# Splitting the row-norm sums and reordering the opening of the feed-forward network in a PE-bound decoder step

## The chip, the cores and the metric

The kernel runs on one core of one Trainium2 chip. The metric is the device time of one execution in microseconds (us). Engines are named as in the profile: PE (TensorE matmul), PEld (its weight loads), DVE (VectorE), ACT (ScalarE), POOL (GpSimd) and SP (the engine that issues most of the DMAs).

## The reference: what is computed

One inference step for 1024 prompt tokens and 32 new tokens (8 sequences of 4), so R = 1056 rows of width D = 1024, float32. Layer 0 is a spatial-gating layer, layer 1 a stick-breaking attention layer; each is followed by a SwiGLU network with 2816 hidden columns. Every sub-layer is preceded by an RMSNorm.

```python
def rmsnorm(x, g):
    r = lax.rsqrt(jnp.mean(xf * xf, axis=-1, keepdims=True) + NORM_EPS)
    return (xf * r).astype(x.dtype) * g

def swiglu(x, wg, wu, wd):
    return (jax.nn.silu(x @ wg) * (x @ wu)) @ wd

def sgu_mixer(xn, w_in, v_g, ws, bs, w_out, chunk_len):
    z = jax.nn.gelu(xn @ w_in, approximate=False)
    u, v = jnp.split(z, 2, axis=-1)
    v = rmsnorm(v, v_g)
    ...
    s = jnp.einsum('gts,bnsgd->bntgd', w, vc) + bs[:, :chunk_len].T[None, None, :, :, None]
    y = (u * s.reshape(B, T, D_MODEL)) @ w_out
```

## The kernel before

**Layout.** Activations lie transposed: 128 features on the partitions, the 1056 rows along the free dimension, eight such tiles for D. Each product is done in three matmuls with split operands (high times high, high times low, low times high), so a tile of 128 output features over 1056 rows is 8 x 3 x 3 = 72 matmuls of 352 columns in `project_from` (L1146). The five engines run five hand-written instruction lists, each strictly in order, tied by counting semaphores (`wait_ge`). PSUM has six banks `ps` (two sets of three) and two banks `aux`.

**Row norms.** The squares of a row lie over 8 x 128 features. ACT squares the tiles, DVE adds the eight squared tiles up in `scratch`, PE sums over the partitions by a matmul with `neg_ones`, 352 columns each, three of them (`row_sums`, the matmul is L1160), alternating between the two `aux` banks. ACT takes the square root of each back into `scratch` (`rms`, L1823, which gives `aux_out`), and DVE takes the reciprocal. As there are two `aux` banks, `aux_free` makes the third sum wait for ACT's first square root. Each of these sums is float32 and shows in the trace as two matmul records.

**The spatial-gating layer.** PE makes tiles 0 to 7 (the v half), then tile 8 (u of group 0), then `row_sums(1)`, tile 9 (u of group 1, bank set 1), tile 10 (u of group 2, bank set 0), then `v_to_rows(0)` and `v_to_rows(1)`: transposes of the normalised v of a group into `aux` in three rounds (L1171 eight transposes in two rounds, L1173 the last), which ACT copies away (`rows_out`, L1832 and L1835); then `spatial` of group 0, which writes bank set 1. DVE's list here is: `scaled_out(8)` (L2446), the reciprocal `r_v` (L2440), eight instructions L2480 that scale the eight v tiles (two big inputs, `v_all` and `r_v`, both in SBUF), then `scaled_out(9)`, `scaled_out(10)`. ACT's list: `gelu_u(0)`, `rms(1)`, `gelu_u(1)`, which waits for `scaled_out(9)`, and only then the copies of `v_to_rows(0)`. The third round of `v_to_rows(0)` needs the copy of its first.

**POOL's weight slabs.** POOL splits each weight slab in three instructions (L1018, L1019, L1022, inputs in SBUF). There are two slots: the slab for tile 11 + x overwrites the slot of a tile that is done, so the split of the next u slab begins as soon as PE ends tile 9, and the one after it as soon as PE ends tile 10.

**The feed-forward network.** It is done in units u = 0, 1, 2, ... (gate and up alternate), each as seven half-size products m = 1 to 7 (a Strassen-like scheme). `product(u, m, bank, fresh)` is 4 x 2 x 3 = 24 matmuls of 264 columns (L1318) into one of four bank pairs; weights come from a ring of seven slots, whose sums DVE makes (`turn_1` to `turn_4`, L2599 to L2619; for the first units `turn_2_alone`, L2635 and L2636), ACT rounds (`part_high`, L1969) and POOL subtracts (`part_low`, L1065). The right-hand sides of m = 5, 6, 7, 3 are sums S1 to S4 of activations that DVE makes in the opening (`q11_made`, `s2_made` L2812, `s3_made` L2819, `s4_made` L2825), ACT rounds (`s_high`, L1989) and DVE subtracts (`s_low`, L2833). DVE also evacuates the banks: `c11_scaled` (L2770), `t6_added` (L2742), `t3_added` (L2747), `c22_added` (L2755), `c12_added` (L2775). In the opening, `product(0, 6)` waits for `c11_scaled(0)`, `product(1, 6)` for `c11_scaled(1)`, `product(0, 7)` for `t6_added(0)`, and `product(2, 6)` for the weight sum that ACT rounds behind `s_high` of S4, tile 2. The opening runs twice, once per layer, with row sums 2 and 4.

Of the kernel before, what the change touches and what calls it, by code (L numbers as in the profile page):

```python
# [33 lines left out]
NC = 3  # L34
CH = R // NC
# [13 lines left out]
Q_SGU, Q_WOUT = 0, 16  # L49
# [27 lines left out]
X_NORM = [3 + 2 * RT + 1]  # L77
# [117 lines left out]
def parted_at(layer, u, m):  # L195

    return NPR * layer + PARTS.index((u, m)) + 1
# [53 lines left out]
def s_low_at(layer, x, j):  # L251

    return 4 * HK * layer + S_LOWS.index((x, j)) + 1
# [21 lines left out]
def a_ready(layer, n):  # L275

    return (2 + 3 * layer) * KT + max(h_order(layer).index(x) for x in range(n + 1)) + 1
# [17 lines left out]
def yoco_step(nc, x_prompt, x_sample, cache_k, cache_v, page_table, norm_mix_g, a_w_in, a_v_g, a_ws, a_bs, a_w_out,  # L295
# [4 lines left out]
    with ExitStack() as ctx:  # L300
        def sb(name, shape, dt=F32, where=ctx):
            return where.enter_context(nc.sbuf_tensor(name, shape, dt))

        def sem(name):
            return ctx.enter_context(nc.semaphore(name))
# [20 lines left out]
        scratch = sb("scratch", [P, R])  # L326
# [13 lines left out]
        neg_ones = sb("neg_ones", [P, P])  # L340
# [36 lines left out]
        in_hi = sb("in_hi", [P, KT, R], F32R, far)  # L377
        in_lo = sb("in_lo", [P, KT, R], F32R, far)
# [87 lines left out]
        aux = ctx.enter_context(nc.psum_tensor("aux", [P, 2, TB], F32))  # L466
# [18 lines left out]
        aux_done = sem("aux_done")  # L485
# [107 lines left out]
        def slot(q):  # L593

            return w_hi[:, q % 2], w_lo[:, q % 2]
# [15 lines left out]
        def ring_slot(layer, u, m):  # L611

            n = PARTS.index((u, m)) % RING
            if n < 4:
                return ring_own[layer][:, n, 0], ring_own[layer][:, n, 1]
            if n < 6:
                x = (w_hi, w_lo)[n - 4][:, last_slot(layer)]
                return x[:, 0:HW], x[:, HW:2 * HW]
            return ring_last[layer][:, 0], ring_last[layer][:, 1]
# [17 lines left out]
        def moving_of(layer, m):  # L637

            if m in (1, 2, 4):
                x = (1, 2, 4).index(m)  # L640
                return A_HI[layer][:, x], A_LO[layer][:, x]
            return s_parts(layer, {5: 1, 6: 2, 7: 3, 3: 4}[m])
# [477 lines left out]
        def _(pe):  # L1120
            mm = nc.tensor.matmul

            def bank_free(t):

                if not isinstance(t, int) or t >= 2:
                    pe.wait_ge(tile_out, t - 1)

            def project(t, par, q, slab, first_input=None, source=(in_hi, in_lo)):

                pe.wait_ge(w_ready, q + 1)  # L1130
                project_from(slot(slab), t, par, first_input, source)

            def project_from(parts, t, par, first_input=None, source=(in_hi, in_lo)):

                bank_free(t)
                hi, lo = parts
                out = ps[:, 3 * par:3 * par + 3, :]
                for k in range(KT):
                    if first_input == 40:
                        pe.wait_ge(in_ready, 40 + max(O_ORDER.index(n) for n in range(k + 1)) + 1)  # L1140
                    elif first_input is not None:
                        pe.wait_ge(in_ready, first_input + k + 1)
                    ks = slice(k * P, k * P + P)
                    for c in range(NC):
                        for n, (w, x) in enumerate(((hi, source[0]), (hi, source[1]), (lo, source[0]))):
                            last = mm(out[:, c, 0:CH], w[:, ks], x[:, k, c * CH:c * CH + CH],  # L1146
                                      start=(k == 0 and n == 0), stop=(k == KT - 1 and n == 2))
                last.then_inc(tile_done, 1)

            def aux_free(x):  # L1150
                if not isinstance(x, int) or x >= 2:
                    pe.wait_ge(aux_out, x - 1)

            def row_sums(event):

                pe.wait_ge(sq_added, KT * event)
                for c in range(NC):
                    x = X_NORM[event] + c
                    aux_free(x)
                    mm(aux[:, x % 2, 0:CH], neg_ones[:], scratch[:, c * CH:c * CH + CH],  # L1160
                       start=True, stop=True).then_inc(aux_done, 1)

            def to_rows(src, x, par):

# [15 lines left out]
            for r in range(RT):  # L1180
                pe.wait_ge(x_in_s[r], 16)
                for n in range(2):
                    x = X_ROWS + 2 * r + n
# [6 lines left out]
            x = X_ROWS + 2 * RT  # L1190
# [8 lines left out]
            for n in range(2):  # L1199
                x = X_WS + n  # L1200
# [5 lines left out]
            near_in = (near_hi, near_lo)  # L1206
# [3 lines left out]
            for rnd in range(NC):  # L1210
                x = X_NORM[0] + rnd
# [8 lines left out]
                for c in range(2):  # L1220
                    project(2 * i + c, c, Q_SGU + 2 * i + c, Q_SGU + c, source=near_in)
            project(8, 0, Q_SGU + 8, Q_SGU + 8, source=near_in)
            row_sums(1)
            project(9, 1, Q_SGU + 9, Q_SGU + 9, source=near_in)

            def v_to_rows(g, par):
                pe.wait_ge(v_normed, g + 1)
# [71 lines left out]
            def ffn(layer, event, t_before):  # L1299
                t0 = T_FFN[layer]  # L1300
                pairs = (ps[:, 0:2], ps[:, 2:4], ps[:, 4:6], aux[:, 0:2])

                def product(u, m, bank, fresh):

                    pe.wait_ge(part_ready, parted_at(layer, u, m))
                    hi, lo = ring_slot(layer, u, m)
                    x_hi, x_lo = moving_of(layer, m)
                    for k in range(HK):
                        if u < 2 and m == 1:
                            pe.wait_ge(in_ready, a_ready(layer, k))  # L1310
                        elif u < 2 and m in (2, 4):
                            pe.wait_ge(in_ready, a_ready(layer, HK + k))
                        elif u < 2:
                            pe.wait_ge(s_ready, s_low_at(layer, {5: 1, 6: 2, 7: 3, 3: 4}[m], k))
                        ks = slice(k * P, k * P + P)
                        for c in range(2):
                            for n, (w, x) in enumerate(((hi, x_hi), (hi, x_lo), (lo, x_hi))):
                                last = mm(pairs[bank][:, c, 0:QC], w[:, ks], x[:, k, c * QC:c * QC + QC],  # L1318
                                          start=(fresh and k == 0 and n == 0), stop=(k == HK - 1 and n == 2),
                                          skip_group_check=True)  # L1320
                    last.then_inc(mult_done, 1)
# [11 lines left out]
                product(0, 1, 0, True)  # L1333
                pe.wait_ge(tile_out, t_before + KT)
                product(1, 1, 1, True)
                row_sums(event)
                product(0, 4, 2, True)
                pe.wait_ge(aux_out, X_NORM[event] + NC)
                product(1, 4, 3, True)
                copied(0)  # L1340
# [441 lines left out]
            for i, n in enumerate(O_ORDER):  # L1782
# [11 lines left out]
                for k in range(first_k, KT):  # L1794
# [4 lines left out]
                    for m, (w, x) in enumerate(((hi, in_hi), (hi, in_lo), (lo, in_hi))):  # L1799
                        for c in range(NC):  # L1800
                            last = mm(out[:, c, 0:CH], w[:, ks], x[:, k, c * CH:c * CH + CH],  # L1801
                                      start=(k == first_k and m == 0), stop=(k == KT - 1 and m == 2))
# [613 lines left out]
        def _(dve):  # L2416
# [34 lines left out]
            for r in range(RT):  # L2451
                for n in range(2):
                    x = X_ROWS + 2 * r + n
# [3 lines left out]
            x = X_ROWS + 2 * RT  # L2457
# [157 lines left out]
            def turn_3(layer, u):  # L2615

                b11, b21, b12, b22 = sources(layer, u)
                dve.wait_ge(turned_done, turned_sum(layer, u, 6 if u < 2 else 5))
                vec.tensor_tensor(b12, b22, b12, ALU.subtract).then_inc(turned_done, 1)  # L2619
# [10 lines left out]
            def turn_2_alone(layer, u):  # L2630

                b11, b21, b12, b22 = sources(layer, u)
                x = ring_sum(layer, u, 6)
                ring_wait(layer, u, 6)
                step_done(vec.tensor_tensor(x, b12, b11, ALU.subtract))  # L2635
                vec.tensor_tensor(x, b22, x, ALU.subtract).then_inc(turned_done, 1)  # L2636
# [48 lines left out]
            def ffn(layer, event, first_in):  # L2685
                t0 = T_FFN[layer]
                r1, ratio, r2 = r_row[:, 0:H2], r_row[:, H2:R], scratch[:, H2:R]
                a, b, c, d = (ps[:, 0:2, 0:QC], ps[:, 2:4, 0:QC], ps[:, 4:6, 0:QC], aux[:, 0:2, 0:QC])
# [78 lines left out]
                def c11_scaled(u, p12):  # L2767
                    a21_read(u, 0)
                    done(u, 2)
                    vec.tensor_tensor(c_of(u, 0), p12, halved(r1), ALU.mult).then_inc(evac, 1)  # L2770
# [56 lines left out]
                def s_low(x, j):  # L2827
                    dve.wait_ge(s_hi_done, s_part_at(layer, x, j))
                    if x == 2:
                        dve.wait_ge(s_ready, s_low_at(layer, 1, j))  # L2830
                    hi, lo = s_parts(layer, x)
                    src = s_sum(layer, 4 if x == 2 else x, j)
                    vec.tensor_tensor(lo[:, j, :], src, as32(hi[:, j, :]), ALU.subtract).then_inc(s_ready, 1)  # L2833
# [4 lines left out]

                for j in range(HK):
                    s_low(1, j)  # L2840
                for j in range(HK):
                    q11_made(j)
                    s2_made(j)
                    if j > 0:
                        s_low(2, j - 1)
                turn_2_alone(layer, 1)
                s_low(2, HK - 1)
                c11_scaled(0, a)
                turn_3(layer, 0)
                s3_made(0)  # L2850
                c11_scaled(1, b)
                turn_3(layer, 1)
                t1_scaled(0)
                t1_scaled(1)
# [63 lines left out]
                for i in range(FP - 1):  # L2918
                    for n in range(KT):
                        t = t0 + KT * i + n  # L2920
# [427 lines left out]
```

## Time and profile before

| | us |
|---|---|
| median of 3 runs | 2614.57 (2613.02 to 2615.01) |
| the profiled execution, its time | 2614.33 |
| its span, first to last instruction | 2612.5 |
| PE busy | 2525.5 (97%) |
| DVE, ACT, POOL busy | 1698.9, 1000.5, 978.7 |
| mean granted TensorE clock | 0.992 |

The span is 1.8 us shorter than the execution's own time. PE is busy nearly all the time, so only a stretch in which PE stands or runs at the lower clock can be won back, and any new one is paid in full.

### The profile page before, as it was taken

Reading aid. Unit: us, or ns where it says so; the run is one execution under the profiler, and the core shown is the slowest. Engines: PE = TensorE matmul, PEld = TensorE weight load, DVE = VectorE, ACT = ScalarE, POOL = GpSimd, SP = SyncE. Lnnn points to the kernel's source line nnn. Section 1 sums busy time; section 2 is a strip of 40 time slices with the busy share of each in tenths; the row PEclk is TensorE's granted clock in tenths of the full one; section 3 lists DMA queues with packets and bytes.
Section 4 is the critical chain, followed back from the end, with each engine's and each line's share of the span. In section 5 each row is a group of like instructions: output and inputs, shape, how many; then the busy total and the mean of one; then the engine's idle time right before and its main releaser. Section 6 shows DMA issues by size and latency. Waiting matters only on the chain.

```text
span 2612.5 us, 44346 instructions
## 1 busy us (share of the span) xinstructions
PE 2525.5 (97%) x17835; PEld 2411.5 (92%) x17835; DVE 1698.9 (65%) x1937; ACT 1000.5 (38%) x1480; POOL 978.7 (37%) x616
## 2 busy tenths in 40 slices
PE   8999989999999999999999999999989999999997
PEld 7989988999999999988888888879889999999997
DVE  4244497556666766778788878885785545567565
ACT  4222153222221111377777777774432222221113
POOL 4643435878985876000000000000245555552110
PEclk9999999999999999999999999999999999999999
DMA  4111223544445664422222231244222222234211
GB/s 132 42 42 34 74 76 96 174 151 158 152 146 216 221 219 152 152 86 84 82 74 80 89 99 61 88 129 160 82 82 82 66 88 77 82 139 162 94 66 75
DMA packets 271134, 284.93 MB, mean 109 GB/s; under 512 B 14810, under 2 KB 213778, under 8 KB 270930
## 3 DMA queue, kind: packets, MB, share of 16 engines
q1 hardware_dynamic: 252770, 272.79, 31.8%
q10 hardware_dynamic: 18160, 9.31, 1.2%
q8 instruction: 141, 2.31, 0.4%
q14 instruction: 63, 0.52, 0.1%
HBM read 195.37 MB, written 86.67 MB: 108 GB/s over the span
## 4 chain that ended last, share of the span: by engine, by line
PE 73%; DVE 10%; issue 3%; ACT 2%; POOL 1%; DMA 1%; ACTq 0%; SPq 0%; DVEq 0%; POOLq 0%
PE ps L1318 24%; PE ps L1407 16%; PE aux L1536 8%; PE aux L1318 4%; PE ps L1146 4%; PE ps L1453 3%; PE ps L1481 3%; PE ps L1435 2%; PE ps L1801 2%; PE ps L1465 2%; DVE s_lo L2833 1%; PE aux L1500 1%; PE aux L1547 1%; DVE h L2924 1%; DVE sp_part_odd L2984 1%
## 5 line engine op out<-in xcount | busy, mean ns | idle before, releaser
L1318 PE MATMUL ps<-s_hi,ring 128*128 128x264 f32 x2016 | 382.0, 287 | 19.1 <-DVE h L2770 8.0
L1065 POOL TENSOR_TENSOR ring<-w_raw,ring 128x512 fp32r<-128x512 f32 x44 | 79.2, 1799 | 844.4 <-ACT ring L1969 844.4
L1318 PEld LDWEIGHTS ps<-s_hi,ring 128*128 128x128 f32 x2016 | 320.4, 191 | 21.7 <-DVE h L2770 8.4
L1407 PE MATMUL ps<-s_hi 128*128 128x352 f32 x1008 | 326.8, 324 | 11.2 <-DVE h L2932 4.5
L1407 PE MATMUL ps<-s_hi,s_lo 128*128 128x352 f32 x1008 | 325.1, 323 | 0.0
L1407 PE MATMUL ps<-s_lo,s_hi 128*128 128x352 f32 x1008 | 323.7, 321 | 0.0
L1318 PE MATMUL ps<-s_lo,ring 128*128 128x264 f32 x1008 | 288.9, 287 | 0.0
L2932 DVE TENSOR_TENSOR h<-h,ps 128x1056 f32<-128x1056 f32 x144 | 180.3, 1253 | 144.2 <-PE ps L1407 142.9
L1065 POOL TENSOR_TENSOR ring<-ring_plain,ring 128x512 fp32r<-128x512 f32 x90 | 132.6, 1491 | 270.4 <-DVE w_hi_plain L2613 228.4
L1969 ACT CAST ring<-ring_plain 128x512 fp32r<-128x512 f32 x90 | 52.0, 621 | 435.4 <-DVE ring_plain L2606 432.7
L1407 PEld LDWEIGHTS ps<-s_hi 128*128 128x128 f32 x1008 | 189.0, 187 | 16.0 <-DVE h L2932 7.9
L1318 PEld LDWEIGHTS ps<-s_lo,ring 128*128 128x128 f32 x1008 | 193.4, 192 | 0.0
L1146 PE MATMUL ps<-near_hi,w_hi 128*128 128x352 f32 x576 | 187.3, 325 | 4.7 <-DVE near_lo L2423 4.7
L1407 PEld LDWEIGHTS ps<-s_hi,s_lo 128*128 128x128 f32 x1008 | 190.4, 189 | 0.0
L1407 PEld LDWEIGHTS ps<-s_lo,s_hi 128*128 128x128 f32 x1008 | 189.6, 188 | 0.0
L2003 ACT CAST s_hi<-a_plain 128x2112 fp32r<-128x2112 f32 x22 | 43.3, 1967 | 381.0 <-PE ps L1407 335.2
L1146 PE MATMUL ps<-near_hi,w_lo 128*128 128x352 f32 x576 | 187.3, 325 | 0.0
L1146 PE MATMUL ps<-near_lo,w_hi 128*128 128x352 f32 x576 | 187.2, 325 | 0.0
L1536 PE MATMUL aux<-in_hi,w_hi 128*128 128x384 f32 (+1 forms) x528 | 172.7, 327 | 1.5 <-issue 0.7
L1536 PE MATMUL aux<-in_lo,w_hi 128*128 128x384 f32 (+1 forms) x528 | 170.3, 322 | 0.0
L1536 PE MATMUL aux<-in_hi,w_lo 128*128 128x384 f32 (+1 forms) x528 | 169.8, 322 | 0.0
L1318 PE MATMUL ps<-a_hi,ring 128*128 128x264 f32 x736 | 142.4, 286 | 4.0 <-DVE h L2770 3.5
(386 smaller groups left out, 6843.9 us busy)
## 6 DMA issues: line engine op xcount, KB each, us to landing
hid_kept<-h SPq DMA_DIRECT2D x44, 528.0 KB, 6.1
a_plain<-hid_kept SPq DMA_DIRECT2D x44, 528.0 KB, 5.5
w_raw<-in_w_gate_dram SPq DMA_DIRECT2D x44, 512.0 KB, 4.9
w_hi<-kept_hi SPq DMA_DIRECT2D x30, 512.0 KB, 4.0
w_lo<-kept_lo SPq DMA_DIRECT2D x30, 512.0 KB, 5.3
h_kept<-h SPq DMA_DIRECT2D x24, 528.0 KB, 3.4
h<-h_kept SPq DMA_DIRECT2D x24, 528.0 KB, 6.4
w_raw<-in_w_down_dram SPq DMA_DIRECT2D x24, 512.0 KB, 4.4
```

The source lines that it names most:

```text
L1065: gp.tensor_tensor(lo, src, as32(hi), ALU.subtract).then_inc(part_ready, 1)
L1146: last = mm(out[:, c, 0:CH], w[:, ks], x[:, k, c * CH:c * CH + CH], start=(k == 0 and n == 0), stop=(k == KT - 1 and n == 2))
L1318: last = mm(pairs[bank][:, c, 0:QC], w[:, ks], x[:, k, c * QC:c * QC + QC], start=(fresh and k == 0 and n == 0), stop=(k == HK - 1 and n = ...
L1407: last = mm(out[:, c, 0:CH], w[:, ns], x[:, c * CH:c * CH + CH], start=(f == 0 and m == 0), stop=(f == 1 and m == 2))
L1435: last = mm(ps[:, e, c0:TB], kq[rows, c, kn, P * j:P * j + P], kq[rows, c, qn, TB * b + c0:TB * b + TB], start=(m == 0), stop=(m == 2 and ...
L1453: last = mm(ps[:, 2 + e, c0:TB], neg_tri_r[:], sp_parts[s % 2][:, x, e, c0:TB], start=(first and x == 0), stop=(x == 1), skip_group_check= ...
L1465: last = mm(ps[:, 2 + e, c0:TB], neg_rest_r[:], sp_parts[s % 2][:, x, e, c0:TB], start=False, stop=(x == 1), skip_group_check=True)
L1481: last = mm(ps[:, 4 + e, c0:TB], v_part[:, j, 2 * e:2 * e + 2, :].rearrange("p n d -> p (n d)"), a_part[:, x, e, c0:TB], start=(first and ...
L1536: last = mm(xb[:, 0:CW[chunk]], w[:, ks], x[:, k, cols], start=(k == 0 and m == 0), stop=(k == KT - 1 and m == 2), skip_group_check=True)
L1801: last = mm(out[:, c, 0:CH], w[:, ks], x[:, k, c * CH:c * CH + CH], start=(k == first_k and m == 0), stop=(k == KT - 1 and m == 2))
L1969: nc.scalar.copy(hi, src).then_inc(part_hi, 1)
L2932: vec.tensor_tensor(chunks(h[:, n, :]), chunks(h[:, n, :]), out, ALU.add).then_inc(tile_out, 1)
```

## The change

Two edits. First, `row_sums` can now issue two of its three sums, and the third is issued from inside the product that follows: in tile 9 of the spatial-gating layer before k = 3 (after 27 of its 72 matmuls), and in `product(0, 4)` of both feed-forward openings before k = 2 (after 12 of its 24). Row sums 3 stay as they are. Second, in DVE's list of the feed-forward opening `c11_scaled(0)` and `turn_2_alone(1)` go from behind the S2 rounds to ahead of them, and `turn_3(0)` goes behind `c11_scaled(1)`.

```diff
-            def project_from(parts, t, par, first_input=None, source=(in_hi, in_lo)):
+            def project_from(parts, t, par, first_input=None, source=(in_hi, in_lo), sum_within=None):
...
                 for k in range(KT):
+                    if sum_within is not None and k == 3:
+                        row_sum(sum_within, 2)
...
-            def row_sums(event):
+            def row_sum(event, c):
+
+                x = X_NORM[event] + c
+                aux_free(x)
+                mm(aux[:, x % 2, 0:CH], neg_ones[:], scratch[:, c * CH:c * CH + CH],
+                   start=True, stop=True).then_inc(aux_done, 1)
+
+            def row_sums(event, count=NC):
 
                 pe.wait_ge(sq_added, KT * event)
-                for c in range(NC):
-                    x = X_NORM[event] + c
-                    aux_free(x)
-                    mm(aux[:, x % 2, 0:CH], neg_ones[:], scratch[:, c * CH:c * CH + CH],
-                       start=True, stop=True).then_inc(aux_done, 1)
+                for c in range(count):
+                    row_sum(event, c)
...
-            row_sums(1)
-            project(9, 1, Q_SGU + 9, Q_SGU + 9, source=near_in)
+            row_sums(1, 2)
+            project(9, 1, Q_SGU + 9, Q_SGU + 9, source=near_in, sum_within=1)
...
-                def product(u, m, bank, fresh):
+                def product(u, m, bank, fresh, sum_within=None):
...
                     for k in range(HK):
+                        if sum_within is not None and k == 2:
+                            row_sum(sum_within, 2)
...
-                row_sums(event)
-                product(0, 4, 2, True)
+                row_sums(event, 2)
+                product(0, 4, 2, True, sum_within=event)
...
                 for j in range(HK):
                     s_low(1, j)
+                c11_scaled(0, a)
+                turn_2_alone(layer, 1)
                 for j in range(HK):
                     q11_made(j)
                     s2_made(j)
                     if j > 0:
                         s_low(2, j - 1)
-                turn_2_alone(layer, 1)
                 s_low(2, HK - 1)
-                c11_scaled(0, a)
-                turn_3(layer, 0)
                 s3_made(0)
                 c11_scaled(1, b)
+                turn_3(layer, 0)
                 turn_3(layer, 1)
```

## Rows read from the trace of the kernel before

**Rows 1.** The page, busy time of each engine

```profile
PE 2525.5 (97%) x17835; PEld 2411.5 (92%) x17835; DVE 1698.9 (65%) x1937; ACT 1000.5 (38%) x1480; POOL 978.7 (37%) x616
```

**Rows 2.** PE's waits, whole span: total us, times, longest

```profile
PE ps L1318 <- DVE h L2770: 11.5, 8, 4.0
...
PE aux L1160 <- ACT scratch L1823: 5.6, 3, 3.1
...
PE aux L1173 <- ACT sgu_row L1832: 2.4, 8, 0.3
```

**Rows 3.** PE's timeline between tiles 8 and 9: start, us, engine, line

```profile
134.11 1.35 PE L1160 MATMUL aux<-scratch,neg_ones 128*128 128x352 f32 x4
138.61 0.88 PE L1160 MATMUL aux<-scratch,neg_ones 128*128 128x352 f32 x2 [3.15 <-ACT scratch L1823]
```

**Rows 4.** Windows after it: PE, PEld, DVE, ACT, POOL busy, clock, DMA

```profile
138.60:139.60 1.00, 0.99 (x4) 0.78 (x5) 0.00 (x0) 0.48 (x2) 1.00 (x1) 0.86 0.00 0
139.60:140.60 1.00, 1.00 (x5) 1.00 (x5) 0.49 (x1) 0.98 (x2) 1.00 (x1) 0.50 0.00 0
...
142.60:143.60 1.00, 1.00 (x8) 1.00 (x7) 1.00 (x1) 0.00 (x0) 0.00 (x0) 0.94 1.10 331
```

**Rows 5.** DVE's timeline over tiles 9 and 10

```profile
140.10 6.75 DVE L2440 RECIPROCAL r_v<-scratch 128x1056 f32<-128x1056 f32 x1 [4.54 <-ACT scratch L1823]
146.89 15.34 DVE L2480 SCALAR_TENSOR_TENSOR v_all<-v_all,gains,r_v 128x1056 f32<-128x1056 f32 x8
162.16 1.25 DVE L2446 TENSOR_TENSOR ev<-ps,r_row 128x1056 f32<-128x1056 f32 x1
164.19 1.26 DVE L2446 TENSOR_TENSOR ev<-ps,r_row 128x1056 f32<-128x1056 f32 x1 [0.78 <-PE ps L1146]
```

**Rows 6.** ACT's timeline over the same stretch

```profile
139.52 0.55 ACT L1823 ACTIVATE scratch<-aux,eps 128x352 f32<-128x352 f32 x1 [0.52 <-PE aux L1160]
...
163.44 1.10 ACT L1878 ACTIVATE u_t<-ev 128x1056 f32<-128x1056 f32 x1 [22.07 <-DVE ev L2446]
164.53 1.07 ACT L1832 COPY sgu_row<-aux 128x512 f32<-128x512 f32 x2
```

**Rows 7.** PE's timeline behind tile 10

```profile
163.89 1.03 PE L1171 MATMUL aux<-ident,v_all 128*128 128x128 f32 x8
165.16 0.28 PE L1173 MATMUL aux<-ident,v_all 128*32 128x128 f32 x1 [0.24 <-ACT sgu_row L1832]
```

**Rows 8.** POOL's timeline over tiles 9 to 11

```profile
152.68 2.21 POOL L1018 TENSOR_TENSOR w_hi<-w_raw,gains 128x1024 fp32r<-128x1024 f32 x1 [12.06 <-PE ps L1146]
154.85 2.91 POOL L1019 TENSOR_TENSOR w_raw<-w_raw,gains 128x1024 f32<-128x1024 f32 x1
157.84 3.28 POOL L1022 TENSOR_TENSOR w_lo<-w_raw,w_hi 128x1024 fp32r<-128x1024 f32 x1
164.20 1.90 POOL L1018 TENSOR_TENSOR w_hi<-w_raw,gains 128x1024 fp32r<-128x1024 f32 x1 [3.08 <-PE ps L1146]
```

**Rows 9.** Line L2480 in two narrow windows: ns min/median/max, start

```profile
L2480 DVE SCALAR_TENSOR_TENSOR v_all<-v_all,gains,r_v x1: 1314/1314/1314, 149.4 to 149.4; 128x1056 f32<-128x1056 f32 x1
...
L2480 DVE SCALAR_TENSOR_TENSOR v_all<-v_all,gains,r_v x1: 2947/2947/2947, 155.9 to 155.9; 128x1056 f32<-128x1056 f32 x1
```

**Rows 10.** Windows: the layer-0 opening in two parts, and behind tile 10

```profile
336.00:385.30 49.30, 44.05 (x315) 42.59 (x314) 48.34 (x50) 30.78 (x47) 18.27 (x13) 0.97 0.15 44
385.90:402.30 16.40, 10.15 (x73) 9.00 (x72) 16.12 (x23) 4.69 (x8) 5.38 (x4) 1.00 0.50 128
...
165.10:171.00 5.90, 4.98 (x38) 4.19 (x38) 1.77 (x4) 2.65 (x8) 5.21 (x3) 1.00 0.02 6
```

**Rows 11.** PE's timeline in the layer-0 opening, two of its waits

```profile
378.52 0.59 PE L1318 MATMUL ps<-s_hi,ring 128*128 128x264 f32 x1 [4.04 <-DVE h L2770]
...
402.35 0.56 PE L1318 MATMUL ps<-s_hi,ring 128*128 128x264 f32 x1 [2.88 <-POOL ring L1065]
```

**Rows 12.** DVE's timeline in the layer-0 opening

```profile
377.77 0.70 DVE L2770 TENSOR_TENSOR h<-ps,r_row 128x528 f32<-128x528 f32 x1
```

More of the change, by code:

```diff
@@ L1126, in bank_free, with project @@
                     pe.wait_ge(tile_out, t - 1)
-            def project(t, par, q, slab, first_input=None, source=(in_hi, in_lo)):
+            def project(t, par, q, slab, first_input=None, source=(in_hi, in_lo), sum_within=None):
                 pe.wait_ge(w_ready, q + 1)
-                project_from(slot(slab), t, par, first_input, source)
-            def project_from(parts, t, par, first_input=None, source=(in_hi, in_lo)):
+                project_from(slot(slab), t, par, first_input, source, sum_within)
+            def project_from(parts, t, par, first_input=None, source=(in_hi, in_lo), sum_within=None):
                 bank_free(t)
```

## The prediction

> **What bounds the kernel now.** I read four views in this order. The page first: PE is busy for 97% of the span [rows 1], so the question is only which of its few stops the change touches, and what ends each. The list of waits names them [rows 2]: three stops of together 5.6 us at the third row sum (L1160, behind ACT's first square root), 11.5 us behind `c11_scaled`, the longest 4.0 us, which is the opening of layer 0, and eight small ones at L1173. Then the timelines of all engines around each stop, because what counts is not who ends the stop but who would end the next one. Last the windows, for the clock.
>
> At the spatial-gating site PE stands for 3.15 us before the third sum [rows 3]. Right after it the granted clock falls to 0.50 (1.2 GHz) [rows 4]: the slice from 138.6 shows 0.86, so the fall lies (1 - 0.86)/0.5 = 0.28 us ahead of its end, at 139.3; the slice from 142.6 shows 0.94, so the rise lies 0.12 us behind its start, at 142.7; the three between show 0.50 (one stands in the group). PE loses half of these 3.4 us, 1.7 us. Taken alone, the edit gives back 3.15 + 1.7 = 4.85 us here and 5.6 - 3.15 = 2.45 us in the two openings.
>
> But see what runs beside it. DVE works without a pause from 140.10 to 163.41 [rows 5]: reciprocal, eight scalings, `scaled_out(9)`. ACT's gelu waits 22.07 us for that last one [rows 6], the copies stand behind the gelu in ACT's list, and PE's third round of transposes waits for the first copy, 0.24 us, at 165.16 [rows 7]. So PE reaches this point already 0.24 us before DVE and ACT let it on. The DVE chain bounds this stretch together with PE; an earlier PE gains nothing here.
>
> **The change part by part: spatial-gating site.** (a) PE's gain up to the end of tile 10: tile 9 is done when POOL starts, at 152.68; tile 10 took 164.20 - 152.68 = 11.52 us [rows 8], that is 0.16 us for each of its 72 matmuls. After the change tile 9 ends at 152.68 - 4.85 = 147.8, tile 10 at 159.35.
>
> (b) The third sum is late. It stood at 138.61. Tile 9 now starts where the first two sums end, about 135.3 (134.11 and four passes, the 1.35 us of the row less the overlap), and the sum comes after 27 x 0.16 = 4.3 us, at 139.6. ACT starts its root 139.52 - 138.61 = 0.91 us behind [rows 3, 6], at 140.5. The reciprocal and all behind it start 1.0 us later. Bounds: 0.7 and 1.4 us, for the end of the sums and the passes in a full pipe.
>
> (c) The collision. An L2480 takes 1.31 us alone and 2.95 us while POOL splits a slab [rows 9]; POOL's L1018 takes 1.90 us when DVE does L2446 and 2.21 us beside L2480 [rows 8]. Neighbours overlap by 0.07 us (146.89 + 15.34 = 162.23, and the next starts at 162.16 [rows 5]), so the free pitch is 1.31 - 0.07 = 1.24 us and eight would take 9.9; they take 15.3. One slab split costs the chain the difference, 5.4 us. Before, exactly one of the two splits fell inside the chain: the first, 152.68 to 161.1. The second started at 164.20, behind the last L2480. After the change the first starts at 147.8, still inside (scalings from 140.10 + 1.0 + 6.79 = 147.9, so again 5.4 us). The chain would then end at 163.2; but the second split now starts at 159.35, with (163.2 - 159.35)/1.24 = 3.1 scalings to go. These three meet its three instructions: another 5.4 us. If the arrival is slightly later in the chain, only two are hit: 2/3 of it, 3.6 us. No hit at all: 0. I take 5.4, as three still fit and in the first split the waiting POOL instruction went ahead of the next scaling.
>
> The Trainium skill, page "SBUF — State Buffer", section "Who interferes with whom", says that a DVE instruction with two SBUF inputs and a GpSimd instruction that reads SBUF exclude one another for a whole instruction, and that one with a single SBUF input does not take part. The trace agrees, with 2.95 against 1.31 us in [rows 9] and an L2446 of 1.26 us (one input in PSUM) beside the split at 164.20. By that rule too, the edit worsens this stretch.
>
> (d) So `scaled_out(9)` ends at 163.41 + 1.0 + 5.4 = 169.8, and gelu, copy and PE's third round move with it: PE resumes 6.4 us later than before, at 171.6 instead of 165.16. Its first eight transposes end at 159.35 + 1.0 = 160.4, so it stands for about 11 us.
>
> (e) The clock. A stop of 3.15 us was followed by 3.4 us at 1.2 GHz [rows 3, 4]; an 11 us stop should be followed by at least as much. The next 5.9 us hold 4.98 us of PE work [rows 10], so half speed is nearly all felt: 1.7 us. Bounds: 0.5 (ACT's copies set the pace) and 3.4 (twice as long).
>
> Sum for this site: 1.0 + 5.4 + 1.7 = 8.1 us slower. Behind it PE is the bound until the opening, so it stays.
>
> **Openings.** (f) The third sum inside `product(0, 4)`: PE gains 1.2 us each. (g) `c11_scaled(0)` used to start at 377.77 and PE's stop ended at 378.52 [rows 11, 12]; it now starts some 9 us earlier. But from 336.0 to 385.3 DVE is busy 48.3 of 49.3 us, and from 385.9 to 402.3 16.1 of 16.4 [rows 10]: a closed queue, with the short dip at 385.6 where it waits for ACT behind `turn_3(1)`. The edit changes the order in that queue, not its sum. `turn_3(1)` ends where it did, so do `t6_added(0)`, which frees `product(0, 7)`, and `s4_made(2)`, behind which ACT and POOL make the weight part that ends PE's stop of 2.88 us at 402.35 [rows 11]. PE's 4.04 us before `product(0, 6)` and the 1.2 us come back as a longer stop before `product(0, 7)`. `product(0, 6)` now also meets the low parts of S2 as they come. Worth: 0. What hides it is DVE's queue; without it the gain would be the rivals' 1.2 + 4.0 us an opening.
>
> (h) Small costs in the queue: `c11_scaled(0)` and `(1)` (one input in PSUM) used to run under POOL's `part_low`; now `s3_made(0)` or the `t1_scaled` meet it, up to 0.6 us an opening, and `s_low(2, 3)` waits some 0.2 us for ACT, as nothing stands between it and `s2_made(3)` any more. I take 0.3 us an opening, 0.6 for the two; bounds -0.5 and +1.5 each, for the clock phase behind 402.35 as well. The second opening shows the same pattern (one of two rows shown).
>
> No DMA is moved and SP's list is unchanged; POOL's is unchanged in order, only its start times move.
>
> **Sum.** 8.1 + 0.6 = 8.7 us. The profiled execution took 2614.33 us, span 2612.5; that makes 2623.0. The median is 0.24 us above it: 2623.3.
>
> **Rivals.** (A) The naive one: PE is the only bound, and its stops vanish. 4.85 + 2.45 = 7.3 us, with `c11_scaled` 8.0 more: 2607.3 down to 2599. For it: PE's 97%. Against it: ACT's 22.07 us wait for DVE and the 0.24 us at L1173. It decides if the copies can come over 1.4 us before 165.16, which ACT's order forbids. It is the case of the other sign. 4%.
> (B) The late sum alone: the second split doesn't meet the scalings (it is late, or the exclusion is looser). 1.0 + 1.7 + 0.6 = 3.3 us: 2617.9. It decides if tile 10 ends behind 162. 14%.
> (C) Two of three scalings are hit: 1.0 + 3.6 + 1.7 + 0.6 = 6.9: 2621.5. 22%.
> (D) The openings do gain, some 1.2 us each, as DVE's queue is not quite closed, on top of my loss: 8.1 - 2.4 = 5.7: 2620.3. 10%.
> (E) The edit does nothing at all that counts: the stops are refilled and the second split harms nothing: 2614.6 to 2616. 5%.
> My own case, 2623.3: 45%.
>
> **Chances and range.** The measurement can tell some 0.2%, 5.2 us, from no change; that threshold is 2619.8. Slower: my case, C and most of D, 0.74. Same: B, E and the rest, 0.22. Faster: A, 0.04. The range takes in C and D, most of B, and above my case the 1.7 us more for the clock and about 1.5 us in the openings: 2617.5 to 2626.5.
>
> **What would show it.** PE has no stop between the L1160 at 134.11 and tile 9; the L1160 inside tile 9 at about 139.6; the last root at 140.5; DVE's eight L2480 take about 20.7 us instead of 15.34, six of them near 2.95 us; POOL's second L1018 starts at about 159.4 and is stretched; PE's stop at L1173 is about 11 us, followed by a clock of 0.50. In the openings the stop before `product(0, 6)` shrinks to under 1 us, the one before `product(0, 7)` grows to some 5 us, and the stretch from tile 7 of the projection to the stop at `product(2, 6)` keeps its length within 1 us. I am wrong if eight L2480 take under 18 us, if PE passes L1173 before 167, or if the openings get shorter.

## The result and the profile after

The changed kernel takes 2625.36 us (median of 6 runs, 2621.45 to 2628.5) against 2614.3 us (6 runs) before; the ratio is 1.0041 with a 95% interval of 1.003 to 1.0052. It is slower by 11.1 us by the medians and by 10.7 us by the ratio; forecast were 8.7 us, 2623.3 us, with a range of 2617.5 to 2626.5. The profiled execution of the changed kernel took 2627.2 us, so its trace has some 2 us that the median has not.

In the new file the lines are shifted: `project_from` is L1148, the transposes are L1177 and L1179, ACT's copies of them L1840, the eight scalings L2488, the evacuations L2454, the products L1326, `c11_scaled` L2778, `t6_added` L2750, the roots L1831. In the experiments the numbers are those of the old or of the new file, or one more.

**The spatial-gating site.** PE's timeline in the changed kernel answers to [rows 3, 7]:

```profile
134.40 1.35 PE L1160 MATMUL aux<-scratch,neg_ones 128*128 128x352 f32 x4
135.32 0.59 PE L1148 MATMUL ps<-near_hi,w_hi 128*128 128x352 f32 x1
...
139.91 0.75 PE L1160 MATMUL aux<-scratch,neg_ones 128*128 128x352 f32 x2
...
159.22 1.03 PE L1177 MATMUL aux<-ident,v_all 128*128 128x128 f32 x8
...
171.59 0.39 PE L1179 MATMUL aux<-ident,v_all 128*32 128x128 f32 x1 [11.34 <-ACT sgu_row L1840]
```

The stop of 3.15 us is gone, tile 9 follows the two sums at once, and the third sum sits inside it. PE is through with tile 10 at 159.2 instead of 163.9. And then it stands for 11.34 us. What it waits for is read from ACT, DVE and POOL in turn; ACT's timeline, answering to [rows 6]:

```profile
140.70 0.56 ACT L1831 ACTIVATE scratch<-aux,eps 128x352 f32<-128x352 f32 x1 [1.40 <-PE aux L1160]
...
169.97 1.08 ACT L1886 ACTIVATE u_t<-ev 128x1056 f32<-128x1056 f32 x1 [27.42 <-DVE ev L2454]
170.97 1.05 ACT L1840 COPY sgu_row<-aux 128x512 f32<-128x512 f32 x2
```

DVE's, answering to [rows 5]:

```profile
141.29 6.75 DVE L2448 RECIPROCAL r_v<-scratch 128x1056 f32<-128x1056 f32 x1 [5.43 <-ACT scratch L1831]
148.08 20.70 DVE L2488 SCALAR_TENSOR_TENSOR v_all<-v_all,gains,r_v 128x1056 f32<-128x1056 f32 x8
168.70 2.41 DVE L2454 TENSOR_TENSOR ev<-ps,r_row 128x1056 f32<-128x1056 f32 x2
```

And POOL's, answering to [rows 8]:

```profile
148.01 1.90 POOL L1018 TENSOR_TENSOR w_hi<-w_raw,gains 128x1024 fp32r<-128x1024 f32 x1 [7.08 <-PE ps L1148]
149.86 2.91 POOL L1019 TENSOR_TENSOR w_raw<-w_raw,gains 128x1024 f32<-128x1024 f32 x1
152.85 3.29 POOL L1022 TENSOR_TENSOR w_lo<-w_raw,w_hi 128x1024 fp32r<-128x1024 f32 x1
159.53 1.95 POOL L1018 TENSOR_TENSOR w_hi<-w_raw,gains 128x1024 fp32r<-128x1024 f32 x1 [3.38 <-PE ps L1148]
161.44 2.90 POOL L1019 TENSOR_TENSOR w_raw<-w_raw,gains 128x1024 f32<-128x1024 f32 x1
164.42 3.23 POOL L1022 TENSOR_TENSOR w_lo<-w_raw,w_hi 128x1024 fp32r<-128x1024 f32 x1
```

Both slab splits now lie beside the scalings (148.08 to 168.78), and the second and third instruction of each are stretched alike; before, the second split began at 164.20 with DVE's scalings done. The scalings take 20.70 us, not 15.34. The windows behind the stop show the clock, answering to [rows 4] (PE, PEld, DVE, ACT and POOL busy, clock, DMA share, GB/s):

```profile
160.30:166.00 5.70, 0.00 (x0) 0.00 (x0) 5.70 (x3) 0.00 (x0) 5.62 (x3) 0.76 0.00 0
166.00:171.50 5.50, 0.00 (x0) 0.00 (x0) 5.11 (x3) 1.52 (x3) 1.66 (x1) 0.50 0.33 95
171.50:173.40 1.90, 1.63 (x7) 1.36 (x8) 0.00 (x0) 0.88 (x4) 0.00 (x0) 0.50 0.03 9
173.40:177.00 3.60, 3.60 (x19) 3.37 (x18) 0.00 (x0) 1.21 (x3) 0.00 (x0) 0.51 0.02 5
177.00:179.00 2.00, 1.80 (x14) 1.40 (x13) 1.19 (x2) 0.52 (x2) 0.00 (x0) 1.00 0.00 0
```

The first window, at 0.76, holds the fall, some 3 us into the stop. The clock stays at 0.50 (1.2 GHz) for the rest of the stop and for the first 5.5 us behind it, to 177.

**The opening of layer 0.** PE's stops there, answering to [rows 11]:

```profile
382.30 0.36 PE L1326 MATMUL ps<-s_hi,ring 128*128 128x264 f32 x1 [0.78 <-DVE s_lo L2841]
384.25 0.39 PE L1326 MATMUL ps<-s_hi,ring 128*128 128x264 f32 x1 [1.00 <-DVE s_lo L2841]
386.30 0.39 PE L1326 MATMUL ps<-s_hi,ring 128*128 128x264 f32 x1 [1.06 <-DVE s_lo L2841]
389.55 0.39 PE L1326 MATMUL ps<-s_hi,ring 128*128 128x264 f32 x1 [1.45 <-DVE h L2778]
...
397.10 0.59 PE L1326 MATMUL ps<-s_hi,ring 128*128 128x264 f32 x1 [4.37 <-DVE h L2750]
...
411.79 0.36 PE L1326 MATMUL ps<-s_hi,ring 128*128 128x264 f32 x1 [2.89 <-POOL ring L1065]
```

Before, the stop in front of `product(0, 7)` was a short one:

```profile
387.69 0.39 PE L1318 MATMUL ps<-s_hi,ring 128*128 128x264 f32 x1 [1.68 <-DVE h L2742]
```

The one stop of 4.04 us before `product(0, 6)` is cut up: three short ones at its start and inside it, together 2.84 us, each on the next tile of S2's low part, then one of 1.45 us on `c11_scaled(1)`; and the stop before `product(0, 7)` grows from 1.68 to 4.37 us. The last one, at `product(2, 6)`, is as long as before (2.88). Measured from DVE's addition of tile 6 (336.14 before, 344.64 after, L2680 in the new file) it comes after 67.15 us instead of 66.21; in the second opening, after 67.13 instead of 66.14.

**Where the time went**, each stretch between the same two instructions of both traces: from the evacuation of tile 8 (134.31, now 134.60) to the addition of tile 6 before the first opening 8.2 us more; the first opening 0.9 us, the second 1.0 us. That is 10.1 of the 12.0 us between the spans; 0.3 lies ahead of tile 8. The remaining 1.6 us lie where the two programs are the same: 0.5 between the openings (from the stop at `product(2, 6)` to the addition of tile 6 in layer 1: 1447.9 before, 1448.4 after) and 1.1 behind the second (696.1 and 697.2). Over all nine traces of this document these two stretches take 1445.6 to 1450.8 and 695.5 to 697.9 us, and the program is the same there in all of them. So nothing shows that the 1.6 us belong to the change, and sums over the edited stretches are a firmer measure than the spans.

### The profile page after: what moved, and what is told of

Its sections match the earlier page's. It is cut to its first block, busy times and chain, and to the rows that moved or that the text cites. A ratio compares the mean times of both kernels' runs of the same rounds, so it can differ in the third digit from the quotient of the medians.

```text
span 2624.5 us, 44346 instructions
## 1 busy us (share of the span) xinstructions
PE 2530.0 (96%) x17835; PEld 2417.4 (92%) x17835; DVE 1705.8 (65%) x1937; ACT 1001.1 (38%) x1480; POOL 983.2 (37%) x616
## 4 chain that ended last, share of the span: by engine, by line
PE 80%; DVE 11%; issue 3%; ACT 2%; DMA 2%; POOL 1%; SPq 0%; ACTq 0%; DVEq 0%; POOLq 0%
PE ps L1326 24%; PE ps L1415 16%; PE ps L1148 10%; PE aux L1544 8%; PE aux L1326 4%; PE ps L1461 3%; PE ps L1489 3%; PE ps L1443 2%; PE ps L1809 2%; PE ps L1473 2%; PE aux L1555 1%; PE aux L1508 1%; DVE v_all L2488 1%; DVE s_lo L2841 1%; DVE h L2932 1%
## 5 line engine op out<-in xcount | busy, mean ns | idle before, releaser
L1326 PE MATMUL ps<-s_hi,ring 128*128 128x264 f32 x2016 | 383.0, 288 | 23.1 <-DVE h L2750 8.7
L1326 PEld LDWEIGHTS ps<-s_hi,ring 128*128 128x128 f32 x2016 | 320.9, 191 | 26.1 <-DVE h L2750 9.2
L1415 PE MATMUL ps<-s_hi 128*128 128x352 f32 x1008 | 327.9, 325 | 10.6 <-DVE h L2940 4.3
L1326 PE MATMUL ps<-s_lo,ring 128*128 128x264 f32 x1008 | 289.0, 287 | 0.0
L1326 PEld LDWEIGHTS ps<-s_lo,ring 128*128 128x128 f32 x1008 | 193.4, 192 | 0.0
L1148 PE MATMUL ps<-near_hi,w_hi 128*128 128x352 f32 x576 | 187.5, 326 | 3.6 <-DVE near_lo L2431 3.6
L1148 PE MATMUL ps<-near_hi,w_lo 128*128 128x352 f32 x576 | 187.2, 325 | 0.0
L1148 PE MATMUL ps<-near_lo,w_hi 128*128 128x352 f32 x576 | 187.1, 325 | 0.0
L1326 PE MATMUL ps<-a_hi,ring 128*128 128x264 f32 x736 | 143.3, 286 | 3.7 <-DVE h L2778 3.6
```

The costliest lines, as they stand in the source:

```text
L1415: last = mm(out[:, c, 0:CH], w[:, ns], x[:, c * CH:c * CH + CH], start=(f == 0 and m == 0), stop=(f == 1 and m == 2))
```

## The experiments

Six kernels were timed against the kernel before, 6 to 12 executions each, and one was executed once. Each left one trace. Each starts from the kernel before; those with a third sum inside a product take `row_sum` and the argument `sum_within` from the change.

**The spatial-gating edit alone**

```diff
-            row_sums(1)
-            project(9, 1, Q_SGU + 9, Q_SGU + 9, source=near_in)
+            row_sums(1, 2)
+            project(9, 1, Q_SGU + 9, Q_SGU + 9, source=near_in, sum_within=1)
```

> Only the spatial-gating edit (the third sum inside tile 9), the feed-forward openings as before. Theory (the eight scalings on DVE meet both slab splits of POOL): the eight scalings take 20.7 us instead of 15.3, PE stands 11.3 us ahead of its third round of transposes and then runs at a clock of 0.50; the kernel is 8.0 us slower than before (6.5 to 9.5). Rival 1 (the loss sits in the openings): within 2 us of before. Rival 2 (PE alone is the bound, and the loss comes from elsewhere): 4.8 us faster.

Measured: 2622.9 against 2614.63 us, ratio 1.0031 (1.0019 to 1.0043). The scalings take 20.70 us and PE's stop is 11.33 us, to 0.01 us the values of the changed kernel. So by the medians this edit alone makes 8.3 of the 11 us (5.0 to 11.2 by the interval); its trace is 6.9 us longer from the evacuation of tile 8 to the addition of tile 6. Rivals 1 and 2 are out. The windows behind its stop, which ends at 171.75:

```profile
171.70:174.80 3.10, 2.87 (x13) 2.38 (x14) 0.00 (x0) 1.82 (x5) 0.00 (x0) 0.50 0.02 5
174.80:177.00 2.20, 2.20 (x19) 2.04 (x19) 0.10 (x1) 0.24 (x2) 0.00 (x0) 0.99 0.03 7
```

The clock is back at 174.8, 3.1 us behind the stop; in the changed kernel it took 5.5 us.

**The same, with POOL's second split held back**

```diff
+            pool.wait_ge(v_normed, KT)
             for i in range(0, 2):
                 for c in range(2):
                     split(Q_SGU + 12 + c, 2, i, c, G_MIX0, scaled + 2 * i + c + 1)
```

> The run above, and POOL waits for all eight scalings before it splits the slab that follows tile 10, so that its three instructions can no longer meet them. Theory: the scalings take 15.3 us again, DVE's chain ends 1.0 us later than before, PE's stop shrinks from 11.3 to about 5.8 us, the clock still falls to 0.50 behind it; 2.7 us slower than before (1 to 4). Rival (the scalings are slow for another reason, say PE's or ACT's accesses beside them, or the late sum costs it all): as slow as the run above, 8 us.

Measured: 2617.84 against 2614.63 us, ratio 1.0012 (1.0004 to 1.0021), 3.2 us slower; 5.1 us of the loss are gone. Its timelines of DVE, POOL and PE:

```profile
147.79 15.34 DVE L2489 SCALAR_TENSOR_TENSOR v_all<-v_all,gains,r_v 128x1056 f32<-128x1056 f32 x8
```

```profile
163.20 1.90 POOL L1018 TENSOR_TENSOR w_hi<-w_raw,gains 128x1024 fp32r<-128x1024 f32 x1 [7.35 <-DVE v_all L2489]
```

```profile
165.93 0.39 PE L1180 MATMUL aux<-ident,v_all 128*32 128x128 f32 x1 [5.97 <-ACT sgu_row L1841]
```

The scalings are back at 15.34 us, and POOL's L1019 and L1022 of the second split at 1.90 and 2.36 (2.90 and 3.23 in the changed kernel); one wait is all that sets this kernel off from the one above. The collision is the cause of 5.4 us of DVE's chain, and this shows it. What is left in the trace is 1.8 us from tile 8 to tile 6: PE resumes 0.8 us later, and the low clock behind its stop of 5.97 us costs 1.0. PE pays nothing for the late slab there.

**The third sum inside the openings alone**

```diff
-                row_sums(event)
-                product(0, 4, 2, True)
+                row_sums(event, 2)
+                product(0, 4, 2, True, sum_within=event)
```

> Only the third sum inside product(0, 4) of both openings; the spatial-gating site and DVE's order as before. Theory (DVE's queue is closed, so PE's 1.2 us come back at its next stop): PE's stop before product(0, 6) grows from 4.0 to about 5.2 us and the time is that of before, within 0.7 us. Rival (PE is the bound): 2.4 us faster, both stops of 1.2 us gone and nothing in their place.

Measured: 2614.37 against 2614.63 us, ratio 0.9998 (0.999 to 1.0007). PE's stop in the first opening:

```profile
378.53 0.59 PE L1326 MATMUL ps<-s_hi,ring 128*128 128x264 f32 x1 [5.38 <-DVE h L2778]
```

The stop at 378.5 grew from 4.04 to 5.38 us and ends where it ended, 378.53 against 378.52. The 1.2 us won at the sum came back here as 1.3; the second opening has a stop of 5.38 us there too.

**DVE's new order alone** (the last part of the diff, nothing else)

> Only DVE's new order in both openings; all sums as before. Theory: the stop of 4.0 us before product(0, 6) becomes three short ones inside it plus one of 4 to 5 us before product(0, 7), and some 0.8 us an opening are lost because DVE's instructions with two inputs in SBUF now meet POOL where those with one input in PSUM stood: 1.7 us slower (0.8 to 3). Rival 1 (only the order changes, not the sum): within 0.5 us. Rival 2 (an earlier c11 frees PE): up to 4 us an opening faster.

Measured: 2616.97 against 2614.63 us, ratio 1.0006 (0.9997 to 1.0016): 2.3 us slower by the medians, which these runs don't separate from none. The traces do: the first opening takes 67.19 us from the addition of tile 6 to the stop at `product(2, 6)`, the second 67.34, against 66.21 and 66.14 before. Counted from the addition of tile 7, the twelve openings of the six traces with the old order take 53.03 to 53.44 us, and the four with the whole new order (this kernel and the changed one) 54.07 to 54.17. DVE's timeline in the first:

```profile
378.65 1.78 DVE L2819 TENSOR_TENSOR s_plain<-h 128x528 f32<-128x528 f32 x1
380.47 0.71 DVE L2770 TENSOR_TENSOR h<-ps,r_row 128x528 f32<-128x528 f32 x1
381.10 0.68 DVE L2619 TENSOR_TENSOR w_raw<-w_raw 128x512 f32<-128x512 f32 x1
...
382.91 1.81 DVE L2735 TENSOR_TENSOR scratch<-s_plain,r_row 128x528 f32<-128x528 f32 x1
384.65 1.77 DVE L2819 TENSOR_TENSOR s_plain<-h 128x528 f32<-128x528 f32 x1
386.34 1.77 DVE L2833 TENSOR_TENSOR s_lo<-s_plain,s_hi 128x528 fp32r<-128x528 f32 x1
```

and POOL's:

```profile
378.59 1.28 POOL L1065 TENSOR_TENSOR ring<-ring_plain,ring 128x512 fp32r<-128x512 f32 x1 [11.35 <-ACT ring L1969]
382.51 1.65 POOL L1065 TENSOR_TENSOR ring<-w_raw,ring 128x512 fp32r<-128x512 f32 x1 [2.64 <-ACT ring L1969]
384.12 1.73 POOL L1065 TENSOR_TENSOR w_hi<-w_lo_plain,w_hi 128x512 fp32r<-128x512 f32 x1
385.82 1.73 POOL L1065 TENSOR_TENSOR w_lo<-w_raw,w_lo 128x512 fp32r<-128x512 f32 x1
```

Four instructions with both inputs in SBUF take 1.77 to 1.81 us where 0.7 is their time, each beside one POOL subtraction; both `c11_scaled` (L2770, one at 380.47) and both `turn_3` (L2619, one at 381.10) run free, with no POOL subtraction beside them. In the order of before, `c11_scaled(0)` at 377.77 and `c11_scaled(1)` at 380.43 each covered part of a subtraction (377.96 and 380.51), and the `turn_3` behind them took only 1.39 and 1.29 us:

```profile
378.39 1.39 DVE L2619 TENSOR_TENSOR w_raw<-w_raw 128x512 f32<-128x512 f32 x1
...
381.06 1.29 DVE L2619 TENSOR_TENSOR w_lo_plain<-w_lo_plain 128x512 f32<-128x512 f32 x1
```

The other two of the four were slow before as well, the `s3_made` at 1.80 us and the `s_low` behind it at 1.14 after 0.57 us of waiting for ACT, so it is the first two that the order lost.

**The new order, with turn_3(0) back in its place**

```diff
                 s_low(2, HK - 1)
+                turn_3(layer, 0)
                 s3_made(0)
                 c11_scaled(1, b)
-                turn_3(layer, 0)
                 turn_3(layer, 1)
```

> DVE's order of the change in both openings, but turn_3(0) back ahead of s3_made(0); all sums as before. Theory (the loss of an opening is which DVE instruction meets POOL): c11_scaled(1) again runs beside POOL's part of (0, 7), so turn_3(1) and the t1_scaled meet less; the stop at product(2, 6) comes 0.3 to 0.8 us later than in the kernel before instead of 1.1. Rival (the loss is the late s_low of S2): 1.1 us later, as with the whole order.

In its one execution, from the addition of tile 6 (335.59) to the stop at `product(2, 6)`, at 402.21, it takes 66.62 us, and 66.63 in the second opening. That is 0.4 us above before and 0.6 below the whole order, as the collisions ask for: the `t1_scaled` take 0.70 us each again, since POOL now works beside `c11_scaled(1)`. Counted from tile 7 it is 53.57 and 53.58 us, clear of the whole order, but only 0.1 above the slowest of the old one. The lines of DVE and of POOL:

```profile
380.30 0.71 DVE L2770 TENSOR_TENSOR h<-ps,r_row 128x528 f32<-128x528 f32 x1
...
382.75 0.70 DVE L2735 TENSOR_TENSOR scratch<-s_plain,r_row 128x528 f32<-128x528 f32 x1
```

```profile
380.37 1.29 POOL L1065 TENSOR_TENSOR ring<-w_raw,ring 128x512 fp32r<-128x512 f32 x1 [1.27 <-ACT ring L1969]
```

**The spatial-gating edit, with tiles 9 and 10 evacuated early.** If PE's time was lost because the gelu, the copies and the next bank hang on evacuations that stand behind all eight scalings, it must come back when these are moved forward.

```diff
                                          r_v[:], ALU.mult, ALU.mult).then_inc(v_normed, 1)
-            scaled_out(9, 1, ev[:, 1, :])
+                if g == 1:
+                    scaled_out(9, 1, ev[:, 1, :])
+                if g == 4:
+                    dve.wait_ge(u_act, 1)
+                    scaled_out(10, 0, ev[:, 0, :])
...
-                    dve.wait_ge(u_act, 2 * i + c + 1)
-                    scaled_out(10 + 4 * i + 2 * c, 0, ev[:, c, :])
+                    if i + c > 0:
+                        dve.wait_ge(u_act, 2 * i + c + 1)
+                        scaled_out(10 + 4 * i + 2 * c, 0, ev[:, c, :])
```

> The third sum inside tile 9, and DVE evacuates tile 9 behind the second of the eight scalings and tile 10 behind the fifth, instead of both behind the eighth; openings as before. Theory (PE's early arrival was lost because the gelu, the copies and the next bank hang on evacuations that stand behind all scalings): both slab splits still meet the scalings, but nothing waits for their end; PE has no stop of over 0.5 us between 134 and 180 us and no clock of 0.50 there; tile 12 begins 4.6 us earlier than in the kernel before, and the kernel is 4.5 us faster than before (3 to 5.5). Rival (another wait takes over, spatial of group 1 on the late gated(0), or the clock): within 1.5 us of before.

Measured: 2608.23 against 2614.51 us, ratio 0.9981 (0.9972 to 0.999): faster than both kernels. By the medians it gains 6.3 us on the kernel before (2.6 to 7.3 by the interval; 3 to 5.5 were expected) and some 17 us on the changed one, though these two were not timed side by side. DVE's timeline, POOL's at the first evacuation, and PE's:

```profile
146.91 5.82 DVE L2488 SCALAR_TENSOR_TENSOR v_all<-v_all,gains,r_v 128x1056 f32<-128x1056 f32 x2
152.65 1.24 DVE L2454 TENSOR_TENSOR ev<-ps,r_row 128x1056 f32<-128x1056 f32 x1
153.82 4.75 DVE L2488 SCALAR_TENSOR_TENSOR v_all<-v_all,gains,r_v 128x1056 f32<-128x1056 f32 x3
158.49 1.25 DVE L2454 TENSOR_TENSOR ev<-ps,r_row 128x1056 f32<-128x1056 f32 x1
159.66 8.00 DVE L2488 SCALAR_TENSOR_TENSOR v_all<-v_all,gains,r_v 128x1056 f32<-128x1056 f32 x3
```

```profile
151.69 3.30 POOL L1022 TENSOR_TENSOR w_lo<-w_raw,w_hi 128x1024 fp32r<-128x1024 f32 x1
```

```profile
159.33 0.28 PE L1179 MATMUL aux<-ident,v_all 128*32 128x128 f32 x1 [0.24 <-ACT sgu_row L1840]
```

The scalings still meet both splits: 5.82 + 4.75 + 8.00 = 18.6 us in all. But nobody waits for their end now; PE passes L1179 with its old 0.24 us, and the stop and the low clock are gone. From the evacuation of tile 8 to the addition of tile 6 it takes 196.9 us (133.44 to 330.32), against 201.8 before: 5.0 us less, close to the 4.85 us that the prediction set down for the edit taken alone. The span is shorter still, by 7.4 us; the other 2.4 lie outside the edited stretch.

**The early evacuation alone**, with all three sums ahead of tile 9

> Only DVE's early evacuation of tiles 9 and 10; all three sums ahead of tile 9 as before. Theory: PE's stop of 3.15 us and the clock loss behind it stay, only the 0.24 us at L1173 go; the time is that of before, within 0.7 us. Rival (DVE's chain alone was the bound, the sums did not matter): as fast as the run above.

Measured: 2615.94 against 2614.51 us, ratio 1.0002 (0.9993 to 1.0011); PE's 3.15 us are there as before. One thing that was expected did not come: the 0.24 us at L1173 did not go. ACT's copy and PE's third round:

```profile
163.17 1.07 ACT L1832 COPY sgu_row<-aux 128x512 f32<-128x512 f32 x2 [9.57 <-PE aux L1171]
```

```profile
163.81 0.28 PE L1173 MATMUL aux<-ident,v_all 128*32 128x128 f32 x1 [0.24 <-ACT sgu_row L1832]
```

ACT now stands idle before the copy and waits for PE alone, and PE still waits 0.24 us for the copy. It resumes 30.9 us behind the evacuation of tile 8 (132.93), to 0.1 us as in the kernel before. So the 0.24 us are there even when nothing but PE's own first transposes holds up the copy, and they are no sign of DVE's chain.

Neither half gives anything by itself, and the two together some 5 us: PE's stop and DVE's chain ended at nearly the same moment, and only taking both away moves the end. How near, three traces say. In the kernel before, the copy starts 0.64 us behind the first transposes (163.89 and 164.53), straight behind the gelu; here, where the gelu is long done, also 0.64 (162.53 and 163.17). And in the run with POOL held back DVE's chain starts 0.9 us later than before and PE resumes 0.8 us later. DVE and ACT were ready 0.1 us ahead of PE.

## Why the prediction was right, step by step

- The reading that DVE's chain bounds this stretch together with PE, so that an earlier PE gains nothing: right, as the two runs with early evacuation show. The number that it was read from was the wrong one. The 0.24 us at L1173 stand there with the chain out of the way as well; the good evidence was ACT's own row, where the gelu's end at 164.54 and the copy's start at 164.53 leave no room.
- (a) PE's gain to the end of tile 10: right. POOL, which starts there, starts at 159.53 against 159.35 forecast.
- (b) The late sum: ACT stands 1.40 us before the third root, which comes 0.9 us later in relation to tile 8 (1.0 forecast).
- (c) The collision: 20.70 us for the eight scalings, to the tenth what was forecast, 5.4 us more. All three remaining scalings met the split, so rivals B and C are out; holding POOL back takes these 5.4 us off the scalings again. The rule of the Trainium skill ("SBUF — State Buffer", "Who interferes with whom"), that a DVE instruction with a single SBUF input stays out of this exclusion, holds here too: in the run with early evacuation L2454, whose other input is in PSUM, takes 1.24 us at 152.65, beside POOL's L1022.
- (d) PE resumes at 171.59 (171.6 forecast), 6.1 us later than before if both are counted from tile 8, where 6.4 were forecast. That the two times of day agree to 0.01 us is luck: the whole trace runs 0.3 us late at tile 8.
- (e) The clock: 1.8 us lost behind the stop (1.7 forecast), and 0.8 us in the run with this edit alone, after the same stop of 11.3 us. What differs is how long the clock stayed at 0.50 behind it, 5.5 and 3.1 us. The mechanism is right and both lie in the forecast's bounds (0.5 and 3.4), but that 1.8 came so near 1.7 is luck too.
- (f) The sums in the openings: 0, as forecast; the 1.2 us came back at the next long stop.
- (g) `c11_scaled` early: the stop before `product(0, 7)` grew as forecast, from 1.68 to 4.37 us against "some 5". Neither part of the edit made an opening shorter, so A and D are out, and E by the interval of the result.
- (h) The small cost was the step that was mis-sized: 0.3 us an opening were forecast, 0.9 and 1.0 measured, within the bounds set (-0.5 and +1.5). I had counted that a `c11_scaled` no longer covers POOL, but only for one of POOL's subtractions; both lost their cover, so that the two subtractions cost DVE 1.1 us each instead of 0.7 and 0.6 (the experiment with DVE's order alone, and the one with `turn_3(0)` back, which takes 0.6 us less again).

The sum of what the trace shows is 8.2 (6.14 at PE's stop, 1.84 for the clock, 0.23 in the same stretch further on) + 0.9 + 1.0 = 10.1 us, with the two openings at 1.9 instead of 0.6; the forecast had 8.7. The 0.23 us are within what this stretch differs by between the four traces with the old spatial-gating site (201.8 to 202.3 us). The rest, up to the 11.1 us between the medians, lies within what medians of six runs with a spread of 7 us leave open: the spatial-gating edit and DVE's order run alone lost 8.3 and 2.3, together 10.6. Why the unchanged stretches differ from trace to trace was not examined and stays open.

Of the signs named, most came. Two came only by half: POOL's second L1018 was hardly stretched (1.95 us), only the two instructions behind it were; and the stop before `product(0, 6)` is under 1 us (0.78), but with the two inside the product PE stands 2.84 us there. The stretch from tile 7 to `product(2, 6)` was to keep its length within 1 us, and grew by 0.96 and 1.01, at the edge of that.

## What to carry to other kernels

Removing a stop of the busiest engine is worth no more than the time by which the next thing that it waits for is ready ahead of it; here DVE and ACT were ready 0.1 us ahead, so removing 3.15 us of stop and 1.7 us of low clock was worth nothing until the evacuations behind it were moved too. To find that margin, look at the engine that opens the gate and whether it stood idle before it did, and not at the short wait on the busiest engine's side, which can be there either way. Ask also what an earlier engine sets off: PE's early arrival started a slab split that ran into DVE's chain, and 5.4 of the 11 us came from instructions that nobody had moved.

## What the runs showed of the hardware that was not expected

- When DVE's scalings and POOL's splits are both ready, they take turns, one whole instruction each: this is read from the durations, where a scaling of 1.31 us takes 2.94 to 3.45 beside POOL and POOL's 1.90 and 2.36 become 2.9 and 3.3. The first scaling of the changed kernel, at 148.08, takes 2.94 us already, behind a POOL instruction that began 0.07 us before it.
- After the same stop of 11.3 us the loss to the lower clock was 0.8 us in one trace and 1.8 in the other. The stops at `product(2, 6)` behave alike in length but not in when the clock falls: in the first opening of the kernel before it was at 0.50 when PE resumed (the matmul at 402.35 takes 0.56 us), in the changed one it was still at 1.00 from 411.8 to 412.4 (the matmul at 411.79 takes 0.36 us) and at 0.50 from 412.5. Over all nine traces each of the fifteen stops of 2.87 to 2.90 us there was followed by 0.50 within 1.5 us, and none of the three shorter ones (2.13, 2.61 and 2.61 us). So a forecast of such a loss needs a range of at least 1 us a stop.
